# Seven up-projection units of the prompt computed in plain fp32 between the value pages, in a reordered decoder step

## Time and profile before

| | |
|---|---|
| time, median of three | 510.21 us |
| the profiled execution | 507.13 us, span 505.3 us, mean granted clock 0.913 |
| busy | PE 432.7 us (86%), DVE 356.4 (71%), ACT 210.4 (42%), POOL 108.9 (22%) |
| DMA | 124.63 MB, mean 247 GB/s |

### The profile page before, as it was taken

The page is one execution under the profiler, slowest core; times in us unless marked ns, Lnnn a source line. Parts: engine busy times, 40 slices in busy tenths (PEclk is TensorE's granted clock), DMA queues, the critical chain, the costliest instruction groups (busy, mean ns, idle before and its releaser), DMA issues.

```text
span 505.3 us, 9218 instructions
## 1 busy us (share of the span) xinstructions
PE 432.7 (86%) x2759; PEld 351.3 (70%) x2759; DVE 356.4 (71%) x481; ACT 210.4 (42%) x832; POOL 108.9 (22%) x158
## 2 busy tenths in 40 slices
PE   1989988899756677798996899999999996999990
PEld 0368867688542333252584699999999996999990
DVE  0568999999877995412345449999999997243528
ACT  1484746647602402112230456666666553333200
POOL 1000000599940000000000003344333335000003
PEclk9969999989977997958889599999999999799996
DMA  8999999999892999999973026666666584666202
GB/s 304 261 385 382 335 387 387 386 387 367 311 390 87 366 388 395 387 387 387 346 232 90 0 67 185 166 167 185 190 192 179 166 228 122 168 170 183 63 1 86
DMA packets 116234, 124.63 MB, mean 247 GB/s; under 512 B 5831, under 2 KB 74256, under 8 KB 116181
## 3 DMA queue, kind: packets, MB, share of 16 engines
q1 hardware_dynamic: 108912, 108.59, 66.0%
q10 hardware_dynamic: 7296, 15.73, 8.4%
HBM read 121.89 MB, written 2.61 MB: 246 GB/s over the span
## 4 chain that ended last, share of the span: by engine, by line
PE 50%; DVE 13%; SPq 10%; POOL 9%; issue 7%; DMA 7%; ACT 3%; DVEq 0%; ACTq 0%; POOLq 0%
PE ps L1198 13%; PE ps L1199 12%; PE ps L1200 12%; SPq L285 7%; PE ps L975 5%; DVE qk L686 5%; DMA KV<-in_cache_k 4%; POOL ct L425 3%; PE ps L979 3%; DVE T L691 2%; DMA wring<-in_cache_v 2%; POOL cu L426 2%; PE ps L1105 2%; SPq L303 2%; ACT qk L510 1%
## 5 line engine op out<-in xcount | busy, mean ns | idle before, releaser
L859 DVE TENSOR_TENSOR wlo<-KV,whi 128x2048 fp32r<-128x2048 f32 (+1 forms) x30 | 75.2, 2505 | 45.6 <-ACT whi L588 31.8
L1198 PE MATMUL ps<-x1h,whi 128*128 128x264 f32 x352 | 101.1, 287 | 0.2 <-issue 0.2
L1199 PE MATMUL ps<-x1l,whi 128*128 128x264 f32 x352 | 101.1, 287 | 0.0
L1200 PE MATMUL ps<-x1h,wlo 128*128 128x264 f32 x352 | 100.7, 286 | 0.0
L975 PE MATMUL ps<-xT,wring 128*128 128x264 f32 x384 | 90.6, 399 | 6.6 <-DMA wring<-in_w_in 6.1
L975 PEld LDWEIGHTS ps<-xT,wring 128*128 128x128 f32 x384 | 75.2, 197 | 21.0 <-DMA wring<-in_w_in 7.0
L686 DVE TENSOR_TENSOR qk<-KV,qk 128x2048 f32<-128x2048 f32 x32 | 73.3, 2326 | 8.7 <-DMA KV<-in_cache_k 6.1
L510 ACT ACTIVATE qk<-qk 128x64 f32<-128x64 f32 x256 | 61.9, 245 | 34.7 <-DVE qk L686 34.7
L1198 PEld LDWEIGHTS ps<-x1h,whi 128*128 128x128 f32 x352 | 67.4, 192 | 0.2 <-issue 0.2
L1199 PEld LDWEIGHTS ps<-x1l,whi 128*128 128x128 f32 x352 | 67.4, 191 | 0.0
L1200 PEld LDWEIGHTS ps<-x1h,wlo 128*128 128x128 f32 x352 | 67.2, 191 | 0.0
(11 more groups left out here) (146 smaller groups left out, 577.2 us busy)
## 6 DMA issues: line engine op xcount, KB each, us to landing
KV<-in_cache_k SPq DMA_DIRECT2D x128, 256.0 KB, 6.8
KV<-in_w_ffn_up SPq DMA_DIRECT2D x44, 512.0 KB, 4.9
wring<-in_cache_v SPq DMA_DIRECT2D x64, 256.0 KB, 8.0
KV<-in_cache_v SPq DMA_DIRECT2D x64, 256.0 KB, 7.6
wring<-in_w_in ACTq DMA_DIRECT2D x6, 2048.0 KB, 14.8
KV<-in_w_ffn_down SPq DMA_DIRECT2D x8, 1408.0 KB, 7.0
qk<-in_w_out ACTq DMA_DIRECT2D x1, 2048.0 KB, 12.2
out<-rows SPq DMA_DIRECT2D x4, 512.0 KB
```

Of the source, the lines that this page charges most:

```text
L859: nc.vector.tensor_tensor(wlo[s][:, 0:n], w2[s][:, 0:n], whi[s][:, 0:n], ALU.subtract).then_inc(s_lo, 1)
L1198: nc.tensor.matmul(out, wh[k], xh[k], start=k == 0, stop=False)
L1199: nc.tensor.matmul(out, wh[k], xl[k], start=False, stop=False)
L1200: ins = nc.tensor.matmul(out, wl[k], xh[k], start=False, stop=k == n - 1)
```

## The change

It reorders the whole front of the kernel and changes the form of seven of the 22 up units (E = 7).

- **Early units 0 to 6.** For the prompt alone they are plain fp32 products: 256 columns, weights as loaded, no split (`early_half`). Ten of their 14 halves lie between the value slots of samples 3 to 7. ScalarE issues their 14 weight DMAs in its own queue (`load_early`), after it has normalised row tile 0: eight, the second exponential, six, then the evictions of x1. The samples' part of these units is done afterwards: rows of x1 as 32-column weights, the unit's weights as 512 moving columns, in four column groups, then sums and transposes by small matmuls.
- **Late units 7 to 21** are as before, in the split form with 264 columns; 15 instead of 22.
- **Convolution.** ScalarE scales the product's last tap while it evicts (`early_scaled`, `late_scaled`); VectorE adds two taps from PSUM instead of three steps over padded tiles; the samples' convolution is done for all units at once at the end.
- **Prompt heads** move from the value stage into the key scan; the copies that staged q, k and v for them on GpSimd go.
- **Samples' softmax:** ranking on 32 partitions, penalties and distances added by TensorE; the first half is taken in steps between slots 17 and 24 of the scan, the second in the first norm. VectorE sums all four pages of six slots (WHOLE) and ScalarE none of them.
- **Projection.** Both halves of w_out in one product per tile (eight matmuls), in between the value slots of samples 0 and 1 and the last key slots, the attention half on the prompt's columns only; the samples' attention part is added later by a product of their rows.
- **SyncE** loads value slots 0 to 7 each behind a key slot of samples 6 and 7, waiting for the value slot two back; the k and v rows are stored between the keys of samples 5 and 6. w_out is loaded by ScalarE behind z tile 19.

The core of the diff:

```diff
@@ -45,14 +43,16 @@
 GD = GP - 1
 FAR = 1.0e30
 BIG = -1.0e30
-Z_ORDER = (0, 1, 4, 5, 3, 2)
+Z_ORDER = (0, 1, 2, 4, 5, 3)
 STATE_ROWS = 2 * NS
 STACK = STATE_ROWS + 3
-
+E = 7
+NL = FT - E
+WHOLE = (12, 13, 15, 16, 17, 19)
 
...
+            def load_keys(b, s, ids):
+                sp.wait_ge(s_kused, b * SLOTS + (s + 1 - SLOTS))
+                load(pages_k, ids[GP * s:], kv[:, s], s_kv[s])
+
+            def load_values(v, ids):
+                i = value_slot(v)
+                if v < 2:
+                    sp.wait_ge(s_z, 24)
+                elif i < 4 and value_count(v) == 1:
+                    sp.wait_ge(s_kused, (NS - 1) * SLOTS + i + 1)
+                else:
+                    sp.wait_ge(s_vused, (v - 2 if v < 12 else v - 6) + 1)
+                load(pages_v, ids[GP * (v % SLOTS):], value_home(v), s_v[i])
+
...
+                    load_keys(b, s, ids)
+            kvr = rows.rearrange("p r (w d) -> p r w d", w=2)
             sp.wait_ge(s_rowcp, 6)
-            kvr = rows.rearrange("p r (w d) -> p r w d", w=2)
             for w, (dst, dsts) in enumerate(((k_prompt, k_sample), (v_prompt, v_sample))):
                 sp.dma_start(dst[0, 0].rearrange("(r p) h d -> p r (h d)", p=P), kvr[:, :, w, :]).then_inc(s_kvo, 16)
                 sp.dma_start(dsts[0].rearrange("b t h d -> (b t) (h d)"),
                              srows[0:NS, w * DA:(w + 1) * DA]).then_inc(s_kvo, 16)
+            for b in range(6, NS):
+                ids, ids_v = page_ids(b), page_ids(b - 6)
+                for s in range(SLOTS):
+                    load_keys(b, s, ids)
+                    load_values((b - 6) * SLOTS + s, ids_v)
+
+            for b in range(2, NS):
+                ids_v = page_ids(b)
+                for s in range(SLOTS):
...
-                half = w2[s][:, 0:KT * 2 * P].rearrange("p (k a n) -> p k a n", k=KT, a=2)
+            def load_up(v):
+                u, s = E + v, late_slot(v)
+                half = w2[s][:, 0:UNIT].rearrange("p (k a n) -> p k a n", k=KT, a=2)
                 for a in range(2):
-                    sp.dma_start(half[:, :, a, :], wup[:, :, bass.ds(u * P + a * FF, P)]).then_inc(s_wu[s], 16)
-
-            for s in range(2):
-                sp.wait_ge(s_vused, NS * SLOTS - 2 + s)
-                load_up(s, s)
+                    sp.dma_start(half[:, :, a, :], wup[:, :, u * P + a * FF:u * P + a * FF + P]).then_inc(s_wu[s], 16)
+
+            for v in range(2):
+                sp.wait_ge(s_vused, NS * SLOTS - 4 + v)
+                load_up(v)
+            sp.wait_ge(s_vused, NS * SLOTS)
...
+            def load_early(u):
+                if u < 2:
+                    act.wait_ge(s_kused, NS * SLOTS)
+                elif u < 5:
+                    act.wait_ge(s_cvT, 5)
+                    act.wait_ge(s_sc, 8)
+                    act.wait_ge(s_ctps, 1)
+                else:
+                    act.wait_ge(s_mix, KT)
+                for a in range(2):
+                    act.dma_start(early[u][:, :, a, :], wup[:, :, u * P + a * FF:u * P + a * FF + P]).then_inc(s_eu[u], 16)
...
             act.wait_ge(s_kvo, 64)
-            for r in (0, 2):
-                normalise(r, s_xh1, 1)
-
+            normalise(first_rows, 0, s_shift, 1, s_xh1)
+            for u in range(4):
+                load_early(u)
+            exponentials(1)
+            load_early(4)
+            load_early(5)
+            load_early(6)
             for m in range(KT):
                 act.wait_ge(s_b1, m + 1)
-                nc.scalar.activation(x1T[:, m, :], ps[:, 4 + m % 4, 0:R], ACT.Identity, bias=lnT[:, 8 + m:9 + m],
-                                     scale=lnT[:, m:m + 1]).then_inc(s_x1, 1)
...
+            def early_scaled(u):
+                bank = ps[:, u % 4, :].rearrange("p (a n) -> p a n", a=2)
+                act.wait_ge(s_u, 2 * u + 2)
+                if u >= 2:
+                    act.wait_ge(s_f, u - 1)
                 for a in range(2):
...
+                    nc.scalar.activation(U[:, u % 2, a, :], bank[:, a, :], ACT.Copy, scale=tap(u + a * FT, 2))
+                nc.scalar.activation(uptail[:, 0:2, u:u + FT + 1:FT].rearrange("p r a -> p a r"), bank[:, :, TAIL:NPR],
+                                     ACT.Copy).then_inc(s_tl, 1)
+
...
+            def multiply(j):
+                b, s = divmod(j, SLOTS)
+                dve.wait_ge(s_qb, b + 1)
+                dve.wait_ge(s_kv[s], 16 * GP * b + 16 * GP)
+                if j >= 2:
+                    dve.wait_ge(s_red, j - 1)
+                    dve.wait_ge(s_reda, act_sums(j - 1))
+                q = qb[:, b:b + 1, :].to_broadcast([P, GP, DA])
+                nc.vector.tensor_tensor(prod[:, j % 2, :].rearrange("p (g d) -> p g d", g=GP), kv[:, s], q,
+                                        ALU.mult).then_inc(s_kused, 1)
+
+            def reduce(j):
+                b, s = divmod(j, SLOTS)
+                n = GP if j in WHOLE else GD
+                dve.wait_ge(s_kused, j + 1)
+                dst = T[:, b // 4, GP * s:GP * s + n, b % 4 * NH:(b % 4 + 1) * NH]
+                nc.vector.tensor_reduce(dst, prod[:, j % 2, 0:n * DA].rearrange("p (g h d) -> p g h d", h=NH, d=DH),
+                                        AX.X, ALU.add).then_inc(s_red, 1)
+
+            def scan(j):
+                if j + 1 < NS * SLOTS:
+                    multiply(j + 1)
+                reduce(j)
+
+            def head_masked(i):
...
+            def gate_penalties(x):
+                dve.wait_ge(s_gps, x + 1)
+                chain(nc.vector.tensor_copy(G8, ps[0:32, 5, 0:NBLK]))
+                gi = G8.rearrange("q (i o) -> q i o", o=1).to_broadcast([32, NBLK, NBLK])
+                gj = G8.rearrange("q (o j) -> q o j", o=1).to_broadcast([32, NBLK, NBLK])
+                nc.vector.tensor_tensor(beats[:, :, 0, :], gj, gi, ALU.is_gt)
...
+            scan(22)
+            probability_sums(0)
+            scan(23)
+            denominators(0)
+            sample_weights(0)
+            sample_weights(1)
+            scan(24)
+            scan(25)
+            for m in range(4):
+                residual(m)
+                scan(26 + m)
+            masked_values(0)
+            sample_weights(2)
+            residual(4)
...
+            def convolved(u, bank_a, bank_g):
+                for k in (1, 0):
+                    n = NPR - 2 + k
+                    for a, bank in ((0, bank_a), (1, bank_g)):
+                        if k:
+                            dve.wait_ge(s_tl, u + 1 if u < E else E + 2 * (u - E) + a + 1)
+                        else:
+                            dve.wait_ge(s_c1, 2 * u + a + 1)
+                        out = U[:, u % 2, a, 2 - k:NPR]
+                        nc.vector.scalar_tensor_tensor(out, bank[:, 0:n], tap(u + a * FT, k), out, ALU.mult, ALU.add)\
+                            .then_inc(s_c1 if k else s_cv, 1)
+
...
+            def mix_tile(m):
                 if m >= 2:
                     pe.wait_ge(s_r1, m - 1)
-                product(ps[:, m % 2, 0:R], [wo_att[:, k, m * P:(m + 1) * P] for k in range(4)],
-                        [catT[:, k, :] for k in range(4)]).then_inc(s_mix, 1)
-                if m >= 1:
-                    pe.wait_ge(s_r1, m)
-                    to_rows(m - 1).then_inc(s_n1, 1)
-            pe.wait_ge(s_r1, KT)
-            to_rows(KT - 1).then_inc(s_n1, 1)
-            for r in range(3):
+                out = ps[:, m % 2, 0:R]
+                for k in range(4):
+                    nc.tensor.matmul(out, wo_mix[:, k, m * P:(m + 1) * P], catT[:, 4 + k, :], start=k == 0, stop=False)
+                for k in range(4):
+                    ins = nc.tensor.matmul(out[:, 0:NPR], wo_att[:, k, m * P:(m + 1) * P], catT[:, k, 0:NPR],
+                                           start=False, stop=k == 3)
+                ins.then_inc(s_mix, 1)
+
...
+            values(0, 0)
+            values(0, 1)
+            pe.wait_ge(s_wom, 16)
+            pe.wait_ge(s_wo, 16)
+            pe.wait_ge(s_cvT, 5)
+            pe.wait_ge(s_hoc, 4)
+            pe.wait_ge(s_ze, 24)
+            pe.wait_ge(s_ctail, 1)
+            mix_tile(0)
+            values(0, 2)
+            mix_tile(1)
+            values(0, 3)
+            mix_tile(2)
+            first_row_tile(0)
+            values(1, 0)
+            mix_tile(3)
+            first_row_tile(1)
+            values(1, 1)
+            mix_tile(4)
+            first_row_tile(2)
+            pe.wait_ge(s_soft, 1)
+            sample_outputs(0)
...
+            def early_half(u, a):
+                if a == 0:
+                    pe.wait_ge(s_eu[u], 32)
+                    if u >= 4:
+                        pe.wait_ge(s_cv, 2 * (u - 4) + 2)
+                        pe.wait_ge(s_tl, u - 3)
+                product(ps[:, u % 4, a * NPR:(a + 1) * NPR], [early[u][:, k, a, :] for k in range(KT)],
+                        [x1T[:, k, 0:NPR] for k in range(KT)]).then_inc(s_u, 1)
+
+            for h in range(10):
```

(76 more changed lines are left out.)

1468 lines of the change are left out of this document (815 added, 653 removed).

## The result

The changed kernel takes **536.07 us** (median of 4 runs, 535.48 to 538.29) against 511.97 for the kernel before on the same chip (4 runs, 509.79 to 513.89): ratio **1.051**, 95% interval 1.045 to 1.056. The forecast was 522, in a range of 496 to 532. Its likeliest case was the right one (the burst of weight DMAs holds ScalarE, so the kernel gets slower); the time lies 14 us above it and 4 us above the range.

What follows compares the result with a forecast made beforehand. Bound by VectorE's key scan, then DMA value pages, then TensorE from 286 us. Samples' part ending at 344, plus 85.7 late units, 69 down tiles and 18.3 tail gave span 517; plus 4.9, time 522, range 496 to 532.

Steps and rivals of the forecast that it cites:

- likeliest case: Issue burst ahead of the x1 evictions holds ScalarE, x1 at 240; time 522, own range 512 to 532, chance 0.47.
- first projection product: Projection starts at 160 us, bounds 152 and 166, behind scan, heads, about 10 us of ranking wait, and GpSimd's convolution.
- normalised rows: After projection to 204: norm up to its transposes 7 us, second softmax half woven in +1, rows at 212.
- loop of ten halves and 20 slots: Early units under value pages: TensorE bounds, 62.5 us plus 2 for its idle start, to 304.5.
- samples' part: After the loop: four more halves, norm wait, 56 products of 512 columns at 0.228 (12.8), transposes; 39.3 us, to 344.
- 15 late units: Behind the samples' part: TensorE bounds, 15 units at 5.7 us each, 85.7 us.
- down tiles: Behind the late units: 70.4 us before, wait for the split and slow cast both kept, given -1.4, so 69.
- Twelve waits of 1.74 plus 0.8: ScalarE's 14 weight issues ahead of x1, priced from SyncE's blocked issues: 21.7 us, bounds 5.9 and 29.8.
- B: Rival: the 14 issues go through at 0.4 us, x1 at 224; span 501, time 506, chance 0.28.
- C: Faster rival: B, and projection starts at 152 instead of 160; span 493, time 498, chance 0.20.
- C's second condition: Before the projection: the ranking doesn't wait for TensorE, so the projection starts at 152, 8 us earlier.
- D: Rival: likeliest case plus TensorE at the low clock through the samples' stretch, +8; time 530, chance 0.05.

Runs made afterwards that it cites:

- spread form: Kernel after, ScalarE's weight issues spread: units 0 to 2 ahead of the normalised rows, 3 behind x1, 4 to 6 behind silus; 506.33 us, 0.993 of the kernel before.
- one edit that changes no wait: Spread issues, with VectorE's subtraction for the second down tile waiting until GpSimd's last split is done; 510.57 us, 0.997 of the kernel before.
- end edits: Spread issues, samples' first batch one unit earlier, late VectorE subtraction (these two: 502.91 us, 0.988), plus down-weight rounding behind the last scaling (all: 505.35 us, 0.990).

## Why the prediction was right in kind and short in size

By its own steps, in span times:

| step | forecast | measured | adds |
|---|---|---|---|
| first projection product | 160 | 159.05 | |
| normalised rows | 212 | 216.65 | 4.6 |
| 14 issues | 21.7 | 28.3 | 6.6 |
| first early product | 240 | 251.3 | 11.3 so far |
| loop of ten halves and 20 slots | 64.5 | 66.9 | 2.4 |
| samples' part | 39.3 | 33.2 | -6.1 |
| 15 late units | 85.7 | 91.5 | 5.8 |
| down tiles | 69 | 73.6 | 4.6 |
| tail | 18.3 | 18.3 | 0 |

11.3 + 2.4 - 6.1 + 5.8 + 4.6 = 18.0 above the forecast span of 517, and 517 + 18 = 535. The time is only 14 above its forecast: the 4.9 us that the forecast added from a span to the median were 1.3 here (534.8 to 536.07). That is luck.

**The burst: right mechanism, one term too small.** "Twelve waits of 1.74 plus 0.8" was right in its steady pace (ten waits, median 1.75). It was wrong for the first two, 5.54 and 4.36: 9.9 less 3.5 is 6.4 of the 6.6 us. In the kernel after, value pages were still landing then. From 220 to 224 us SyncE's queue moved 0.93 MB and ScalarE's 0.48, from 228 to 232 us ScalarE's moved 1.15 MB alone. The burst of the earlier trace rows, whose third and fourth DMAs waited 2.42 and 1.74 us, had no pages beside it once its first microsecond was over. So the row gave the pace of an undisturbed queue, and the forecast used it for a shared one. The upper bound of 29.8 held, but the range did not take it in.

The Trainium skill (DMA: Bandwidth & Descriptors, "Issuing engines are not separate DMA queues") says that issuing from several engines saves only the sequencer's time, usually small beside the DMA. The two queues did share the DMA engines here, as it says, but the sequencer's time was 28.3 us of an engine on the path.

**The normalised rows** came 4.6 us late, and 3.6 of them lie in the norm. The last projection product ended at 205.0 (forecast 204), and the rows then took 11.6 us and not 8. The forecast gave the second softmax half woven into it 1 us; on VectorE its steps from the ranking to the shifted scores take 4.6 us between 206.5 and 215.2, with another 1.1 us of wait for TensorE.

**Rivals.** B and C, both faster or equal, needed issues of 0.4 us; two of 14 were. With the burst gone the first early product stands at 224.9, where B put x1 at 224, yet B's span of 501 was 508.3: the late units and down tiles were too cheap in it as well. C's second condition came true in part and brought nothing: VectorE waited for TensorE 1.7 and 1.0 us in the whole stretch (forecast 10), yet the first projection product stands at 159.05. D, the low clock through the samples' stretch, did not come (0.98 in that stage); the low clock was in the idle stretch instead (0.51) and cost 1.3 us in the first half unit, 4.96 instead of 3.65. The page burst of 5.73 us in the earlier trace rows, which the forecast puts at clock 0.5, ran at a mean of 0.63.

**The first projection product** came at the forecast time by errors that cancel. VectorE's rows around it:

```profile
155.45 0.51 DVE L881 TENSOR_TENSOR Pw<-T,rden 128x136 f32<-128x136 f32 x2
155.88 2.28 DVE L785 TENSOR_TENSOR qk<-KV,qk 128x2048 f32<-128x2048 f32 x1
163.89 0.42 DVE L892 SCALAR_TENSOR_TENSOR xT<-xT,ps 128x264 f32<-128x264 f32 x1
```

The forecast let the projection wait for the place of the first residual (L892), behind slot 25, and had VectorE there at 147. VectorE got there at 163.9, 17 us later. The scan began 6.2 us later than in the kernel before (first multiplication at 24.70 instead of 18.50), VectorE waited 8.3 us for ScalarE's sums, a term that the forecast does not have (ScalarE itself had waited for TensorE's z products in that stretch), and the heads' masks and maxima took 12.0 us and not 9.2; against that the 6.1 us of waiting for pages, which the old scan had, went. But the first product does not need the residual. In TensorE's order it stands behind value slots 0 and 1, which need the weights of the softmax (L881), ready at 156.0 behind slot 23. So the gate was two slots of keys, 8 us, earlier than the forecast had it, and the ranking's 10 us of wait for TensorE did not come.

**The loop** was 2.4 us longer: a half unit takes 3.65 us and not 3.45, 2.0 us in ten.

**The samples' part** was over-costed: the 56 products take 6.25 us and not 12.8. I priced them by page products that stream 512 columns each; these stream 256, and the section on the change is wrong where it says 512.

**The late units** cost 6.1 us each and not 5.7. The pace of 5.71 came from counting 168 products in 20 us, which counts those that straddle the edges; all 1056 in 130.5 us give 5.93 per unit, start at half clock included. The better row stood in the same sentence. The rest is the start at a granted clock of 0.50 (351.4 to 356), spread over 15 units instead of 22, and a gap of 0.25 us every two units: at clock 1.00 a unit takes 5.96 us here (356.0 to 442.9) and 5.82 in the old stage (291.0 to 416.6).

**The down tiles** were given a gain of 1.4 us against the kernel before and lost 3.2 instead (73.6 against 70.4), 4.6 away from the forecast. "The new order keeps both" (wait and cover) was wrong: the first down product waits for the samples' batch over 20 units, which VectorE and ScalarE only finish behind the last prompt unit. What used to be a wait in the middle of the tile, behind products that covered part of it, became one at its start.

**What the change is worth without the burst.** The spread form is at 0.993 and, with one edit that changes no wait, 0.997: level with the kernel before or a little faster. An early unit takes TensorE 7.3 us in two halves against 6.1 for a late one, the samples' weights and products come on top, and the idle TensorE time under the value pages seems to pay for it, no more. With the end edits it is about 1% faster than the kernel before (0.990, 0.986 to 0.994; 0.988, 0.981 to 0.995, with two of them): a small gain, but clear of the noise.

What stays open: how much room the queue has, in rows or in DMAs, for which one run at another row length is only a hint; why GpSimd, with 14 issues in 12.5 us, was not held; and what the new order is worth without early units.

## What to carry to other kernels

ScalarE and SyncE were held here from about the third outstanding DMA of 512 KB on, until older bytes had moved (GpSimd was not). Price a burst at its bytes over the achieved rate, add the share that other queues take of the DMA engines at that time, and put it where the engine's next instruction is not needed that long, or one pair at a time between other work. Moving the burst to GpSimd freed ScalarE, but the lump of bytes still delayed the pages in SyncE's queue. And when work is split off a stream (here eight sample columns), look where the two halves meet again: the first instruction that needs both inherits the later one.

## What the hardware showed that I had not expected

- ScalarE's queue: DMAs of 512 KB in 512 B rows take 0.37 and 0.60 us for the first two, then 5.54, 4.36 and 1.75 each; beside loading pages up to 7.37 (the spread form).
- GpSimd's queue took the same 14 in 12.5 us, with a landing time of 26.7 us (median of its last four).
- TensorE came back at a granted clock of 0.50 after 26 us without work. In the run with GpSimd's issues it worked at 1.00, stood still for 4.0 us, was at 0.50 behind the gap (259.5 to 265.9 us), and ran the next half unit in 5.15 us and not 3.72.
